# Routed experts of a two-layer transformer block: pairs of 64-row blocks in the two column halves of TensorE, four experts' weights kept, sums in two row sets

## The reference

```python
def _moe(h, w_r, b_r, wg, wu, wd, swg, swu, swd):
    idx, wts = _route(h, w_r, b_r)          # top 8 of 64 experts, weights scaled by 2.5
    return _moe_routed(h, idx, wts, wg, wu, wd) + _swiglu(h, swg, swu, swd)

# _moe_routed, for each token tok and each of its 8 experts e with weight w:
y = (jax.nn.silu(xb @ wg[e]) * (xb @ wu[e])) @ wd[e]
acc.at[tok].add(y * w)
```

## Time and profile before

| | |
|---|---|
| median of 3 runs | 3468.37 us (3464.82 to 3480.79) |
| span of the profiled execution | 3472.4 us |
| profiled span against the median | 4.0 us longer, inside the spread of the runs |
| TensorE busy over the span | 87% |
| mean DMA rate over the span | 185 GB/s |
| first and last addition to `ffn_rows`, layer 0 | 927.7 and 1857.1 us |
| first and last addition, layer 1 | 2579.9 and 3440.5 us |

### The profile page before, as it was taken

The page is one execution under the profiler, slowest core; times in us unless marked ns, Lnnn a source line. Parts: engine busy times, 40 slices in busy tenths (PEclk is TensorE's granted clock), DMA queues, the critical chain, the costliest instruction groups (busy, mean ns, idle before and its releaser), DMA issues. The chain is left out here.

```text
span 3472.4 us, 54592 instructions
## 1 busy us (share of the span) xinstructions
PE 3025.3 (87%) x17979; PEld 2267.7 (65%) x17980; DVE 1300.4 (37%) x3937; ACT 617.2 (18%) x1376; POOL 1162.9 (33%) x1009
## 2 busy tenths in 40 slices
PE   6688979988899999989994698899789999999995
PEld 5365655636577777777773466666457777777774
DVE  5643461524333333323334644524322332233223
ACT  1122231310111111111113122212111111111111
POOL 0766798500121222212222637672111221222122
PEclk9898999997999999999997898999799999999998
DMA  6121212103589888898884211221359999988995
GB/s 218 31 70 37 85 49 96 62 27 112 214 252 322 263 251 287 284 306 272 286 276 141 67 53 31 85 88 39 114 184 312 300 310 295 300 273 245 300 304 161
DMA packets 199258, 642.71 MB, mean 185 GB/s; under 512 B 23296, under 2 KB 117760, under 8 KB 165632
## 3 DMA queue, kind: packets, MB, share of 16 engines
q1 hardware_dynamic: 157264, 520.86, 41.2%
q0 software_dynamic: 41904, 120.67, 16.9%
HBM read 589.19 MB, written 89.03 MB: 195 GB/s over the span
## 5 line engine op out<-in xcount | busy, mean ns | idle before, releaser
L1389 PEld LDWEIGHTS ps<-xT,wgu 128*128 128x128 f32 x9088 | 1033.3, 192 | 116.0 <-issue 115.2
L1389 PE MATMUL ps<-xT,wgu 128*128 128x128 f32 x9088 | 1048.1, 276 | 26.4 <-DVE xT L1473 24.2
L1337 POOL DMA_INDIRECT X<-h_rows,gix x146 | 149.2, 1022 | 1300.8 <-DVE wc L1476 659.5
L1396 PE MATMUL ps<-wd,hidden 128*128 128x512 f32 x1136 | 525.8, 606 | 0.0
L550 PE MATMUL ps<-w_in,hT 128*128 128x512 f32 (+3 forms) x1152 | 396.9, 505 | 15.6 <-PEq L485 4.3
L1396 PEld LDWEIGHTS ps<-wd,hidden 128*128 128x128 f32 x1136 | 209.3, 194 | 215.1 <-issue 212.3
L550 PEld LDWEIGHTS ps<-w_in,hT 128*128 128x128 f32 x1152 | 213.2, 203 | 184.9 <-issue 177.4
L1485 DVE TENSOR_TENSOR hidden<-silu,ps 128x128 f32<-128x128 f32 x284 | 81.5, 287 | 596.7 <-ACT silu L1441 595.4
L1356 POOL DMA_INDIRECT ffn_rows<-Y,six x142 | 226.4, 1595 | 170.8 <-ACT Y L1446 147.7
L1382 PE MATMUL ps<-cst,X 128*128 128x128 f32 x1152 | 162.3, 286 | 99.4 <-DMA X<-h_rows,gix 99.1
L1441 ACT ACTIVATE silu<-ps 128x128 f32<-128x128 f32 x284 | 78.7, 277 | 902.3 <-PE ps L1389 902.3
(11 more groups left out here) (447 smaller groups left out, 3652.4 us busy)
## 6 DMA issues: line engine op xcount, KB each, us to landing
wgu<-in_exp_gu SPq DMA_DIRECT2D x128, 2048.0 KB, 8.9
wd<-in_exp_d SPq DMA_DIRECT2D x128, 1024.0 KB, 7.8
ada_start<-in_ada_w SPq DMA_DIRECT2D x8, 1024.0 KB, 9.7
w_in<-in_w_in SPq DMA_DIRECT2D x4, 2048.0 KB, 8.2
w_in<-in_w_out SPq DMA_DIRECT2D x4, 2048.0 KB, 11.1
aw_0A<-in_ada_w SPq DMA_DIRECT2D x12, 512.0 KB, 3.8
aw_0B<-in_ada_w SPq DMA_DIRECT2D x12, 512.0 KB, 3.9
w_in<-in_w_in SPq DMA_DIRECT2D x2, 3072.0 KB, 10.6
```

The costliest lines, as they stand in the source:

```text
L1337: pool.indirect_dma_start(out=X[j][:, :], out_offset=None, in_=v.h2_dram, in_offset=bass.IndirectOffsetOnAxis(ap=gix[j][:, 0:1], axis=0), ...
L1389: last = pe.matmul(ps[:, f, h * P:(h + 1) * P], wgu[w][:, k, h * FD + f * P:h * FD + (f + 1) * P], xT[:, k, :], start=(k == 0), stop=(k == ...
L1396: last = pe.matmul(ps[:, 5 + c, :], G[:, f, :], wd[w][:, f, c * 512:(c + 1) * 512], start=(f == 0), stop=(f == 1))
```

## The change

- **Blocks of 64.** Rows of an expert are cut into blocks of 64 (`HB`). With the same choice of the router that makes 127 and 93 blocks. A pass takes two consecutive ones, whether of one expert or of two: 64 passes in layer 0 and 47 in layer 1, where the last turn brings them to 48. So 112 passes stand in place of 142.
- **Column halves.** A pass's block h sits in rows 64h to 64h+63 of `X` and in columns 64h.. of `xT`. Now 64 columns of `xT` are stationary and 512 columns of the weights move; the output of block h goes to PSUM partitions 64h.., which places the matmul in that half of the array's columns. Consecutive matmuls alternate between the halves. Gate and up take 16 matmuls (32 records), the down product 8 (16 records).
- **A turn of the hidden units.** The hidden units are now columns, so they are turned by two more transposes (`turn_hidden`) and copied to `G` by ScalarE and VectorE.
- **Four experts' weights** are kept (`NB = 4`). Experts 1 to 3 are loaded when the stage begins. The code of the products exists once for each pair of buffers that can occur, eight times, and `by_buffers` picks one by three nested branches.
- **Two row sets.** One token can be in both halves of a pass, so the upper half adds to rows 768 to 1535 of `ffn_rows` (`second rows`). They are cleared in `route`, and `ffn_residual` loads both sets and adds them (`add_halves`).
- **Signals.** `Y` is no longer held until the last addition has landed: GpSimd signals `y_free` when it is about to issue the next addition. VectorE copies its half of `xT` before it touches `six`. The row of zeros and its store in `load_all` go.

The core of the diff:

```diff
-                def gate_up_products(w):
-                    for f in range(2):
-                        for h in range(2):
-                            for k in range(KD):
-                                last = pe.matmul(ps[:, f, h * P:(h + 1) * P], wgu[w][:, k, h * FD + f * P:h * FD + (f + 1) * P],
-                                                 xT[:, k, :], start=(k == 0), stop=(k == KD - 1))
-                        last.then_inc(gate_up, 1)
+                def gate_up_products(w, landed):
+                    for h in range(2):
+                        pe.wait_ge(w_gu[w[h]], landed[h])
+                    for k in range(KD):
+                        for h in range(2):
+                            last = pe.matmul(ps[h * HB:(h + 1) * HB, 0, :], xT[:, k, h * HB:(h + 1) * HB], wgu[w[h]][:, k, :],
+                                             start=(k == 0), stop=(k == KD - 1))
+                    last.then_inc(gate_up, 1)
...
+                def turn_hidden():
+                    for f in range(2):
+                        last = pe.transpose(ps[:, 6 + f, 0:P], HID[:, f * P:(f + 1) * P], v.ident)
+                    last.then_inc(g_turned, 1)
...
+                def by_buffers(variant, products, landed, a, n):
+
+                    if n == 1:
+                        products((a // 2, (a // 2 + a % 2) % NB), landed)
+                        return
+                    with pe.If(variant < a + n // 2):
+                        by_buffers(variant, products, landed, a, n // 2)
+                    with pe.Else():
+                        by_buffers(variant, products, landed, a + n // 2, n // 2)
...
-                    pe.wait_ge(gathered[(j + 1) % U], turn * 16 + (16 if j == 0 else 32))
-                    turn_rows((j + 1) % U)
+                    pe.wait_ge(gathered[(j + 1) % U], turn * 16 + (16 if j == 0 else 32))
+                    turn_rows((j + 1) % U, 0)
+                    pe.wait_ge(hidden, i + (1 + CREDIT))
+                    turn_hidden()
+                    turn_rows((j + 1) % U, 1)
                     pe.wait_ge(y_act, i + CREDIT)
                     pe.wait_ge(y_dve, i + CREDIT)
...
                     pool.wait_ge(added, i * 16 + 16)
-                    waited()
+                    pool.sem_inc(y_free, 1)
                     pool.indirect_dma_start(out=v.acc_dram, out_offset=bass.IndirectOffsetOnAxis(ap=six[j][:, 0:1], axis=0),
...
+                add_halves(0)
+                add_halves(1)
                 mean_square(0)
                 s_row.wait(dve, 16)
                 for i in range(nt):
+                    if i + 2 < nt:
+                        add_halves(i + 2)
```

More of the change, by code:

```diff
@@ L184, in _ @@
             def _(dve):
[L185 to L194, removed]
+                dve.memset(v.half[:, :], -0.5)
+                dve.memset(v.ones[:, :], 1.0)
             @block.scalar
@@ L1026, in _ @@
                 load_expert(v, sp, l, 0, ex)
+                s_clear.wait(sp, 3)
+                for i in range(nt - 1):
+                    sp.dma_start(v.acc_dram[NROW + i * P:NROW + (i + 1) * P, :], ex.Y[0][:, :]).then_inc(s_zero.sem, 16)
                 s_wt.wait(sp, 1)
@@ L1105, in _ @@
                 s_tab.wait(pe, 1)
-                for c in range(3):
-                    last = pe.matmul(ps[0:1, 0, c * P:(c + 1) * P], tb[:, 3 + c:4 + c], v.ident, start=True, stop=True)
+                for c in range(5):
+                    last = pe.matmul(ps[0:1, 0 if c < 4 else 7, c % 4 * P:(c % 4 + 1) * P], tb[:, c:c + 1], v.ident, start=True, stop=True)
                 last.then_inc(s_tt.sem, 1)
@@ L1287, in sb @@
             return v.sb(f"{n}_{l}", shape, dt, scope=scope)
-        ex.wgu.append(sb("wgu1", [P, KD, 2 * FD]))
-        ex.wd.append(sb("wd1", [P, 2, D]))
+        for w in range(1, NB):
+            ex.wgu.append(sb(f"wgu{w}", [P, KD, 2 * FD]))
+            ex.wd.append(sb(f"wd{w}", [P, 2, D]))
         wgu, wd, X, Y = ex.wgu, ex.wd, ex.X, ex.Y
-        SG, G = sb("silu", [P, 2, P]), sb("hidden", [P, 2, P])
+        SG, HID, G = sb("silu", [P, FD]), sb("hidden", [P, FD]), sb("hiddenT", [P, 2, P])
         xT = sb("xT", [P, KD, P])
-        cur = sb("cur", [P, nt])
+        cur = sb("cur", [P, nt, 2])
         mark = sb("mark", [P, nt, P], F16)
@@ L1394, in down_products @@
                     for f in range(2):
                         for c in range(2):
-                            last = pe.matmul(ps[:, 5 + c, :], G[:, f, :], wd[w][:, f, c * 512:(c + 1) * 512], start=(f == 0), stop=(f == 1))
+                            for h in range(2):
+                                last = pe.matmul(ps[h * HB:(h + 1) * HB, 1 + c, :], G[:, f, h * HB:(h + 1) * HB],
+                                                 wd[w[h]][:, f, c * 512:(c + 1) * 512], start=(f == 0), stop=(f == 1))
@@ L1478, in body, with entries @@
+                def entries(i):
+                    return [entry(dve, T_E0 + h * TABN, i, E - 1) for h in range(2)]
                 def body(i, turn, j):
-                    e1, e2 = entry(dve, 0, i + 1, E - 1), entry(dve, 0, i + 2, E - 1)
+                    e1, e2 = entries(i + 1), entries(i + 2)
                     dve.wait_ge(indexed, i + 2)
-                    mark_slots(i + 2, e2, i * 3 + 7)
-                    for f in range(2):
-                        dve.wait_ge(silu, i * 2 + (f + 1))
-                        dve.wait_ge(down, i + DOWN_CREDIT)
-                        dve.tensor_tensor(G[:, f, :], SG[:, f, :], ps[:, f, P:2 * P], ALU.mult).then_inc(hidden, 1)
@@ L1486, in body @@
-                    dve.wait_ge(added, i * 16 + 16)
-                    dve.tensor_copy(six[j][:, :], gix[j][:, :]).then_inc(y_index, 1)
+                    mark_slots(i + 2, e2, i * 4 + 10)
+                    dve.wait_ge(silu, i + 1)
+                    dve.tensor_tensor(HID[:, :], SG[:, :], ps[:, 0, FD:2 * FD], ALU.mult).then_inc(hidden, 1)
+                    dve.wait_ge(g_turned, i + 1)
+                    dve.wait_ge(down, i + DOWN_CREDIT)
+                    dve.tensor_copy(G[:, 1, :], ps[:, 7, 0:P]).then_inc(g_dve, 1)
```

262 lines of the change are left out of this document (142 added, 120 removed).

## The result

| | before | changed |
|---|---|---|
| median of the runs | 3474.0 us (4 runs) | 3833.5 us (3825.5 to 3842.6, 4 runs) |
| profiled execution: time, span | | 3834.5 us, 3832.6 us |
| ratio to before | | 1.104, 95% interval 1.101 to 1.107 |

The changed kernel is 10% slower. The forecast was 3253 us, 6% faster. Here is the changed kernel's page: the engines' busy time, the row of TensorE's clock among the slices, and a queue of part 3.

A forecast was written before the change was run, and what follows sets the result against it. TensorE was taken to bound the kernel, and DMA to bound layer 1 after the change. 864 + 710 - 1815 + 26 = -215 us turns 3472.4 into 3257; the median is 4 less, 3253 us, range 3160 to 3490.

The forecast's parts named there:

- rival 4: Expert loop outgrows TensorE's instruction store and fetches again every turn; 3533 us at two waits a turn, chance 0.18.
- Layer 0, 13.5 us a pass: TensorE's pass: products 11.4, list and turning 1.63, new wait 0.12, shape changes 0.35; 64 passes, 864 us against 942.
- changes of shape: TensorE switching between 128 and 64 columns, two in a pass: 0.35 us for both, bounds 0 and 0.66.
- late rows: TensorE's waits for gathered rows were to shrink; no gain counted, 0 to 1 us of loss allowed in the range.
- the table reads and branches: TensorE's sequencer reads three entries instead of two, under the down product; 0 to 0.5 us, taken as nothing.
- Products side by side: Two column halves of TensorE's array work together nearly throughout: 11.4 us a pass, bounded by 10.3 and 20.6.
- rivals 2 and 3: Products: other half's weights not loaded ahead, 3426 us, chance 0.12; halves don't run together, 4220 us, chance 0.06.
- rival 1: Near-full overlap of the halves and a well-fed weight queue: products 10.3, pass 12.5 us, total 3160 us, chance 0.12.
- Layer 1, DMA bound, 710 us: DMA transfers become the bound of layer 1's expert loop: between 669 and 746 us, taken as 710.
- Around the loops, +26 us: Outside the loops: `ffn_residual` additions 12 us, first rows and table reads 10, clearing and small `route` steps 4.
- The six waits: VectorE's `six` waits 151 us for the last addition's landing; these waits were to be gone.

The follow-up runs named there:

- shifted kernel: The changed kernel with 215 instructions that only raise an unused semaphore put ahead of TensorE's program; 3266.4 us, ratio 0.940 to the kernel before.
- e9: The shifted kernel with VectorE's `six` and `make_index` moved up between the multiply and the copy of the turned hidden units; 3249.2 us, ratio 0.936.
- e12: e9 with its padding moved to the start of layer 0's expert stage, behind a branch and never run; 3221.5 us, ratio 0.928.
- e5: The kernel before with only `y_free` replacing the wait for the landed addition, and the copy into `xT` ahead of `six`; 3422.9 us, ratio 0.984.
- e13: The kernel before with 750 never-run instructions behind a branch at one place of each pass of TensorE's loop; 3931.1 us.

## Why the prediction was wrong

- **The failed step is the weighing of rival 4**: "Two waits a turn over 56 turns are 280 us: 3533 us", at a chance of 0.18. The mechanism was described rightly, and the rule cited there ("the loop fits barely or misses by one block") was the decisive one. Its price was too small by 3.7 times (18.6 us a turn where 5 were taken), since not two but nearly all blocks are fetched again (7.7 packets a turn, 2.4 us lost for each). And it struck 32 turns, not 56: 32 x 18.6 = 595 us. The forecast itself had this term at nothing. What I used against it, that nothing of the kind was seen in the kernel before, was no evidence: its loops lie in three and four blocks, five with the next, and fit at any place. More could be said ahead of a run: 1,747 instructions lie in 7 blocks at 46 of 256 possible starts and in 8 at the other 210, so a chance of 0.18 was low. Which of the two loops would miss couldn't be told, since the instructions ahead of the program weren't known: the positions in the compiled program alone would have it the wrong way round.
- **Layer 0, 13.5 us a pass:** met once the loop is held, 13.40 us in the shifted kernel, but in part by luck, as two errors of about 1 us cancel. The parts read from its timeline: gate and up to the token list 7.02 us and the down product 3.48, 10.5 together, changes of shape included, where I had 11.4 + 0.35; against that 1.2 us too much stand 2.0 us from the list to the down product where I had 1.75, late rows (0.4 us a pass), and 0.5 to 0.6 us on "issue" ahead of gate and up in every second pass or so, where the table reads and branches stand, which I took as nothing.
- **Products side by side:** right. Two weight loads every 0.43 us, no efficiency lost; rivals 2 and 3 did not occur. The estimate of 1.59 times, from the three column tiles of the Trainium skill ("TensorE: Matmul & The Clock Gate", Part 3), isn't met: here it is 2.0. The products come close to the 10.3 us of rival 1, whose 12.5 us a pass doesn't follow from its own terms (10.3 + 1.63 + 0.12 is 12.05).
- **Layer 1, DMA bound, 710 us:** 701 in the changed kernel and 695 in the shifted one. The DMA isn't the only limit there: moving the index (e9) took another 0.23 us off a pass.
- **Around the loops, +26 us:** +21 in the changed kernel; +26 in e12 (3218.6 - 64 x 13.29 - 48 x 14.26 = 1683.6 us against 1657.4). The sum fits; its parts weren't measured one by one.
- **The six waits:** gone, as said; worth 51 us alone (e5), and late rows came in their place, 0.4 us a pass in layer 0 of the shifted kernel, inside the 0 to 1 allowed.
- With the loops in place the forecast of 3253 us would have met 3266.4 us, or 3243 without the padding's 23 us.

## What to carry to other kernels

When a change copies code into a loop (one copy for each buffer, unrolling), count TensorE's instructions from the loop's start to its end in the compiled program and lay blocks of 256 over them. Here loops of 8 blocks, looking ahead included, were held and those of 9 were not, and 20 instructions ahead of a loop decided. As what runs ahead of the program isn't known, try the loop at a few shifts. TensorE and DMA idle together, waits on "issue" that no row explains, a lower clock and packets on the instruction queue inside a loop are the sign. A jump over never-run padding moves a loop for free, but is a patch, as any later edit shifts it again; fewer copies leave room, though with two buffers in place of four they cost 324 us here.

## What was unexpected of the hardware

- A loop that is one block too long loses nearly all of them: 7 to 11 packets of 16 KB a turn, 1.9 to 2.4 us lost for each, in which TensorE mostly stands still (up to 16.3 us in one wait), and the granted clock is 0.77 to 0.88 in the windows of layer 0.
- Code never run takes no room by itself, but the block behind each piece that is run seems to (e13: 5 blocks, 8 with the next, are held; 6 and 9 are not).
- Two 64-column halves with 512 moving columns run together fully if their instructions alternate (7.09 us for 32 records), and over three or four records if not (12.26 us).
- An instruction that only raises a semaphore took up to 0.2 us of TensorE's queue at the program's start (256 more put off the first addition by 50.6 us, the first 215 by 23).
